# Long convolution of a 768-token mixer: two channel tiles by ScalarE products and adding DMAs, and the layer norm's steps placed between the blocks of the last mixing projection

## What is computed

```python
def conv_mixers(h, w_in, conv_a, conv_b, conv_b_bias, ln_g, ln_b, w_out):
    p = h @ w_in                                   # 1024 -> 5 x 512
    g_b, g_c, u_a, v_b, gate_b = jnp.split(p, ...)
    y_a = g_b * dwconv(g_c * u_a, conv_a)          # 3 taps
    u = v_b * jax.nn.sigmoid(gate_b)
    u = dwconv(u, conv_b) + conv_b_bias            # 31 taps, 512 channels
    y_b = jax.nn.silu(layernorm(u, ln_g, ln_b))    # over the 512 channels
    return jnp.concatenate([y_a, y_b], axis=-1) @ w_out
```

## Time and profile before

| what | value |
|---|---|
| median of 3 runs | 2915.93 us (2907.51 to 2917.44) |
| the profiled execution's own time | 2914.16 us |
| its span, first to last instruction | 2912.0 us |
| mean granted TensorE clock | 0.983 |
| PE busy | 2784.3 us (96%) |
| DVE busy | 1778.3 us (61%) |
| ACT busy | 1115.3 us (38%) |
| adding DMAs (`sw_vb<-tap_prod`) | 29, 391.5 KB each, median 5.2 us from issue to landing |

### The profile page before, as it was taken

The page is one execution under the profiler, slowest core; times in us unless marked ns, Lnnn a source line. Parts: engine busy times, 40 slices in busy tenths (PEclk is TensorE's granted clock), DMA queues, the critical chain, the costliest instruction groups (busy, mean ns, idle before and its releaser), DMA issues.

```text
span 2912.0 us, 41332 instructions
## 1 busy us (share of the span) xinstructions
PE 2784.3 (96%) x14371; PEld 2313.7 (79%) x14371; DVE 1778.3 (61%) x2765; ACT 1115.3 (38%) x1869; POOL 162.4 (6%) x205
## 2 busy tenths in 40 slices
PE   7998999999778999999998999999999998999998
PEld 6886788888676788887887888888888887788886
DVE  6775577676664677767885653453456655564645
ACT  5554322224664322223433332231224666352432
POOL 4211000001110000000210000000000000000000
PEclk8999999999998999999998999999999999999999
DMA  3211355452001344542651112112111000232322
GB/s 129 66 44 66 116 174 181 166 178 75 30 30 58 139 172 166 181 152 71 147 131 44 51 59 72 58 58 69 56 56 44 15 30 18 78 101 87 98 90 66
DMA packets 75217, 263.70 MB, mean 91 GB/s; under 512 B 8496, under 2 KB 10800, under 8 KB 73264
## 3 DMA queue, kind: packets, MB, share of 16 engines
q1 hardware_dynamic: 70880, 249.99, 25.5%
q0 software_dynamic: 4176, 11.63, 2.2%
HBM read 247.87 MB, written 2.10 MB: 86 GB/s over the span
## 4 chain that ended last, share of the span: by engine, by line
PE 67%; issue 16%; DVE 11%; ACT 4%; DVEq 2%; POOLq 0%; POOL 0%; ACTq 0%
PE psum L1942 18%; PE psum L1943 17%; PE psum L1944 17%; PE psum L2092 2%; DVE work L1471 1%; PE psum L2070 1%; PE psum L2341 1%; PE psum L2071 1%; ACT work L1101 1%; PE psum L2072 1%; DVE w_lo L1299 1%; ACT sw_pt L1113 1%; DVE work L1589 1%; DVE neg_max L1832 1%; PE psum L2329 1%
## 5 line engine op out<-in xcount | busy, mean ns | idle before, releaser
L1942 PE MATMUL psum<-hx_hi,w_hi 128*128 128x512 f32 x1568 | 624.6, 398 | 3.8 <-DVE hx_lo L1583 1.2
L1943 PE MATMUL psum<-hx_lo,w_hi 128*128 128x512 f32 x1568 | 622.0, 397 | 0.0
L1944 PE MATMUL psum<-hx_hi,w_lo 128*128 128x512 f32 x1568 | 621.3, 396 | 0.0
L759 ACT ACTIVATE w_hi<-w_raw 128x1024 fp32r<-128x1024 f32 (+1 forms) x328 | 344.8, 1051 | 515.1 <-PE psum L1944 207.5
L1299 DVE TENSOR_TENSOR w_lo<-w_raw,w_hi 128x1024 fp32r<-128x1024 f32 (+1 forms) x328 | 398.2, 1214 | 188.9 <-ACT w_hi L759 170.8
L1944 PEld LDWEIGHTS psum<-hx_hi,w_lo 128*128 128x128 f32 x1568 | 295.1, 188 | 72.0
L1942 PEld LDWEIGHTS psum<-hx_hi,w_hi 128*128 128x128 f32 x1568 | 295.3, 188 | 62.8 <-DVE hx_lo L1583 4.6
L1943 PEld LDWEIGHTS psum<-hx_lo,w_hi 128*128 128x128 f32 x1568 | 295.1, 188 | 47.5
L1942 PE MATMUL psum<-a_hi,w_hi 128*128 128x512 f32 (+1 forms) x656 | 234.6, 358 | 9.5 <-DVE a_lo L1411 9.0
L1943 PE MATMUL psum<-a_lo,w_hi 128*128 128x512 f32 (+1 forms) x656 | 234.5, 357 | 0.0
L1944 PE MATMUL psum<-a_hi,w_lo 128*128 128x512 f32 (+1 forms) x656 | 234.3, 357 | 0.0
(11 more groups left out here) (310 smaller groups left out, 4909.0 us busy)
## 6 DMA issues: line engine op xcount, KB each, us to landing
mod_w<-in_w_mod SPq DMA_DIRECT2D x96, 512.0 KB, 3.7
w_raw<-in_fup SPq DMA_DIRECT2D x88, 512.0 KB, 4.6
w_raw<-in_cup SPq DMA_DIRECT2D x88, 512.0 KB, 3.6
w_raw<-in_fdown SPq DMA_DIRECT2D x32, 512.0 KB, 4.8
w_raw<-in_cdown SPq DMA_DIRECT2D x32, 512.0 KB, 3.6
sw_vb<-tap_prod POOLq DMA_DIRECT2D x29, 391.5 KB, 5.2
w_raw<-in_da_qkv SPq DMA_DIRECT2D x18, 512.0 KB, 3.7
w_raw<-in_fdown SPq DMA_DIRECT2D x16, 384.0 KB, 3.3
```

Source lines behind the costliest of these rows:

```text
L759: r = act.activation(w_hi[:, off:off + n], w_raw[:, raw:raw + n], ACT.Copy)
L1942: pe.matmul(dst, wh, xh, start=first, stop=False)
L1943: pe.matmul(dst, wh, xl, start=False, stop=False)
L1944: return pe.matmul(dst, wl, xh, start=False, stop=last)
```

## The change

Three things are changed.

1. ScalarE and the adding DMAs now do tile 1 (31 taps) and, of tile 3, taps 10 to 30 (`SUM_TILES`). VectorE keeps tiles 0 and 2 and the first 10 taps of tile 3. A table, `PRODUCTS`, gives the products of each of 12 steps: steps 0 to 3 lie behind the last four blocks of `mix_c`, steps 4 to 11 behind the eight blocks of `mix_a`. Steps 0 to 3 have 3 products each, of tile 1; steps 4 to 11 have 6, 6, 6, 5, 5, 4, 4 and 4, of which the first part is of tile 1 and the second of tile 3. Each tile has two sums and 3 product buffers. The first two products of a tile go straight into its sums, the others are added by a DMA, so there are 48 adding DMAs instead of 29.
2. VectorE does 72 taps itself instead of 93, all of them ahead of `mix_b`, and in block 0 of `mix_b` adds up the sums (`conv_sums`) before it evacuates that block.
3. The blocks of `mix_b` are multiplied one after another (`mix_last`), not the first two side by side, in two of the four PSUM areas that blocks otherwise take in turn, and TensorE does the means behind block 0, the squares behind block 1 and the roots behind block 2. The other engines' steps of the layer norm are placed in the evacuation of the same blocks. The output projection takes k in the order 0, 1, 2, 4, 5, 6, 7, 3.

```diff
-SUM_TILE = 1
-TAP_BUFS = 4
+OWN_TAPS = [(q, j) for q, n in ((0, TAPS), (2, TAPS), (3, 10)) for j in range(n)]
+SUM_TILES = {1: 0, 3: 10}
+TAP_BUFS = 3
...
+def product_order():
+
+    steps, at = [], dict(SUM_TILES)
+
+    def take(q, n):
+        got = [(q, j) for j in range(at[q], min(at[q] + n, TAPS))]
+        at[q] += len(got)
+        return got
+
+    for b in range(12):
+        steps.append(take(1, 3 if b < 7 else 2) + (take(3, 3 if b < 9 else 2) if b >= 4 else []))
+    return steps
...
-    layernorm = dict(kind="layernorm", lin0=n["lin"], tile0=n["tile"])
-    stages.append(layernorm)
+    stages.append(dict(kind="layernorm"))
     n["tile"] += 4
-    add("resid", KT_D, k=KT_D, toks=ALL, w="w_out", src="A", gates=(0, 16), squares=ALL, ready=4)
-    layernorm["after"] = stages[-1]
+    add("resid", KT_D, k=KT_D, toks=ALL, w="w_out", src="A", gates=(0, 16), squares=ALL,
+        order=(0, 1, 2, 4, 5, 6, 7, 3))
...
+            return ps_lin(s % 2 if st["kind"] == "mix_b" else s, a, b)
...
-                    for j in range(2, TAPS):
-                        pool.wait_ge(s_tapp, j + 1)
-                        if j >= 4:
-                            pool.wait_ge(s_taps[j % 2], taps_added(j - 2))
-                        pool.dma_start(tap_sum(j % 2), tap_prod[:, j % TAP_BUFS, 0:TAP_COLS], accum_op=ALU.add)\
-                            .then_inc(s_taps[j % 2], 16)
+                    for n, (q, j) in enumerate(PRODUCT_LIST):
+                        at = j - SUM_TILES[q]
+                        if at < 2:
+                            continue
+                        pool.wait_ge(s_tapp, n + 1)
+                        if at >= 4:
+                            pool.wait_ge(s_taps[q][sum_of(q, j)], taps_added(q, j - 2))
+                        pool.dma_start(tap_sum(q, sum_of(q, j)), tap_buf(q, j), accum_op=ALU.add)\
+                            .then_inc(s_taps[q][sum_of(q, j)], 16)
...
+            def tap_products(step):
+
+                for q, j in PRODUCTS[step]:
+                    at = j - SUM_TILES[q]
+                    u = padded(q)[:, j:j + TAP_COLS]
+                    w = vcol("conv_b", TAPS * q + j)
+                    if at >= 2 + TAP_BUFS:
+                        act.wait_ge(s_taps[q][sum_of(q, j - TAP_BUFS)], taps_added(q, j - TAP_BUFS))
+                    dst = tap_sum(q, at) if at < 2 else tap_buf(q, j)
                     if j == 0:
-                        act.activation(dst, u[:, j:j + TAP_COLS], ACT.Identity, scale=w, bias=vcol("conv_b_bias", SUM_TILE))\
-                           .then_inc(s_tapp, 1)
+                        act.activation(dst, u, ACT.Identity, scale=w, bias=vcol("conv_b_bias", q)).then_inc(s_tapp, 1)
                     else:
-                        act.activation(dst, u[:, j:j + TAP_COLS], ACT.Copy, scale=w).then_inc(s_tapp, 1)
+                        act.activation(dst, u, ACT.Copy, scale=w).then_inc(s_tapp, 1)
                     act.drain()
...
-                    tap_products(12 + 3 * b, 15 + 3 * b)
+                    if b == 0:
+                        act.wait_ge(s_ev, st["lin0"] + 4)
+                    tap_products(4 + b)
                 return f
 
             def evac_mix_b(st):
                 def f(b, s, i):
...
             def evac_mix_b(st):
                 def f(b, s, i):
+                    if b == 3:
+                        norm_outputs()
                     act.wait_ge(s_ev, b + (st["lin0"] + 5))
                     act.activation(a_hi[:, b, :], wk[:, 2 * (s % 2), 0:ALL], ACT.Copy).then_inc(s_ahi, 1)
                     act.drain()
+                    if b == 0:
+                        norm_squares()
...
-                    conv_taps(42 + 9 * b // 2, 42 + 9 * (b + 1) // 2)
+                    conv_taps(42 + 30 * b // 8, 42 + 30 * (b + 1) // 8)
...
+            def conv_sums():
+
+                for q, first in SUM_TILES.items():
+                    for c in range(2):
+                        dve.wait_ge(s_taps[q][c], taps_added(q, TAPS - 1 - (TAPS - 1 - first - c) % 2))
+                    parts = [tap_sum(q, 0), tap_sum(q, 1)] + ([wk[:, 3, 0:TAP_COLS]] if first else [])
+                    for a, e, c in segs(ALL):
+                        o = HALO * c
+                        r = dve.tensor_tensor(conv_out[:, q, a:e], parts[0][:, o + a:o + e], parts[1][:, o + a:o + e], ALU.add)
+                    if first:
+                        dve.drain()
+                        for a, e, c in segs(ALL):
+                            o = HALO * c
+                            r = dve.tensor_tensor(conv_out[:, q, a:e], conv_out[:, q, a:e], parts[2][:, o + a:o + e], ALU.add)
+                    r.then_inc(s_ln["conv"], 1)
+                    dve.drain()
...
             def evac_mix_b(st):
+                tile0 = st["tile0"]
+
                 def f(b, s, i):
+                    if b == 0:
+                        conv_sums()
+                    if b == 2:
+                        norm_mean_squares()
+                    if b == 3:
+                        norm_outputs(tile0)
                     t = wk[:, 2 * (s % 2), 0:ALL]
                     dve.wait_ge(s_mm, b + (st["block0"] + 1))
-                    dve.tensor_tensor(t, ps_lin(s), conv_a[:, b, :], ALU.mult).then_inc(s_ev, 1)
+                    dve.tensor_tensor(t, ps_of(st, s), conv_a[:, b, :], ALU.mult).then_inc(s_ev, 1)
+                    dve.drain()
+                    low_part(b, t, ALL, tile0 + (b + 1 if b < 3 else 8))
                     dve.drain()
                     if b == 0:
-                        for c in range(2):
-                            dve.wait_ge(s_taps[c], taps_added(TAPS - 1 - c))
-                        for a, e, c in segs(ALL):
-                            o = HALO * c
-                            r = dve.tensor_tensor(conv_out[:, SUM_TILE, a:e], tap_sum(0)[:, o + a:o + e],
-                                                  tap_sum(1)[:, o + a:o + e], ALU.add)
-                        r.then_inc(s_ln["conv"], 1)
-                        dve.drain()
-                    low_part(b, t, ALL, b + (st["tile0"] + 1))
-                    dve.drain()
-                    conv_taps(78 + 4 * b, min(82 + 4 * b, 93))
+                        norm_centers()
...
-                pair(st["after"], 0, 4)
+            def norm_means():
...
+            def mix_last(st):
+                for s, inside in enumerate((norm_means, norm_squares, norm_roots, None)):
+                    pe.wait_ge(s_lo, st["block0"] + s + 1)
+                    pe.wait_ge(s_ev, st["lin0"] + (s + 1 if s < 2 else s + 3))
+                    for k in range(KT_D):
+                        step(st, s, k)
+                    if s == 0:
+                        pe.wait_ge(s_ev, st["lin0"] + 4)
+                    if inside is not None:
+                        inside()
...
+                    if st["before"]["kind"] == "mix_b":
+                        pe.wait_ge(s_ev, st["lin0"] + 4)
+                for at in range(k0, k1):
+                    k = st["order"][at] if st.get("order") else at
+                    operand(st, at)
```

More of the change, by code:

```diff
@@ L54 @@
 ROW, ROW_N = offsets(ROW_COLS)
+def product_order():
[7 more added lines that the diff above has]
+    return steps
+PRODUCTS = product_order()
+PRODUCT_LIST = [tap for step in PRODUCTS for tap in step]
+assert len(PRODUCT_LIST) == sum(TAPS - first for first in SUM_TILES.values())
 def make_plan():
@@ L188, in program @@
         w_raw = sbuf("w_raw", [P, 4 * D])
+        tap_space = ExitStack()
+        _, tap_prod3, _, tap_sum3 = (sbuf(name, shape, F32, tap_space) for name, shape in (
+            ("tap_gap", [P, 4 * D]), ("tap_prod3", [P, 2, D]), ("tap_gap2", [P, 4 * D]), ("tap_sum3", [P, 2, D])))
+        tap_space.close()
         w_hi = sbuf("w_hi", [P, 6 * D], F32R)
@@ L311, in program @@
         s_tapp = sem("tap_product_ready")
-        s_taps = [sem(f"tap_added_to_sum{c}") for c in range(2)]
+        s_taps = {q: [sem(f"tap_added_to_sum{c}_of_tile{q}") for c in range(2)] for q in SUM_TILES}
         s_const = sem("constants_ready")
@@ L892, in f @@
                         act.drain()
[L893 to L897, removed]
-                return f
[L900 to L904, removed]
-                    act.activation(wk[:, j % 2, 0:ALL], conv_out[:, j, :], ACT.Square).then_inc(s_ln["sq"], 1)
-                    act.drain()
-                for j in range(4):
-                    act.wait_ge(s_ln["t"], j + 1)
-                    act.activation(wk[:, 2 + j % 2, 0:ALL], wk[:, j % 2, 0:ALL], ACT.Silu,
-                                   bias=vcol("ln_bias", j)).then_inc(s_ln["s"], 1)
-                    act.drain()
-                    act.activation(a_hi[:, 4 + j, :], wk[:, 2 + j % 2, 0:ALL], ACT.Copy).then_inc(s_ahi, 1)
-                    act.drain()
+                    if b == 4:
+                        act.wait_ge(s_ev, st["lin0"] + 8)
+                    if b >= 4:
+                        tap_products(b - 4)
```

(15 more changed lines are left out.)

59 lines of the change are left out of this document (38 added, 21 removed).

## The result

| what | before | changed |
|---|---|---|
| median | 2915.99 us (4 runs) | 2953.80 us (4 runs, 2947.93 to 2956.61) |
| ratio to before, 95% interval | | 1.0129 (1.0113 to 1.0145) |
| the profiled execution: time, span, clock | 2914.16, 2912.0, 0.983 | 2955.53, 2953.6, 0.974 |

The changed kernel is 37.8 us slower by the medians; the forecast was 2951 us, 35 us above the median of before (36.9 above its profiled execution). The mixer stage takes nearly all of it: from the root of the norm ahead of it to the root of the norm behind it (POOL's `tok_r`) it lasts 318.9 us instead of 284.2 us.

A forecast was written before the change was run, and what follows sets the result against it. TensorE set the pace up to 1520 us; after the change the DMA engines bound `conv_out`, whole at 1537.5 us. Plus 70.4 us, the pair ends at 1607.9, 36.9 later: 2914.2 + 36.9 = 2951 us, range 2933 to 2970.

The forecast's parts named there:

- The price of an add: Each adding DMA within SBUF occupies all 16 DMA engines for 2.26 us.
- The last add: Behind mix_a's blocks, the last adding DMA lands at 1535.3 us, at a DMA share of 1.03.
- an engine works at one packet at a time: Reading of the DMA share, never much above 1.09 in the busiest slices.
- Late weights: Roundings queue behind products, so TensorE stalls some 7 us in mix_a or at mix_b; costed at nothing.
- From `conv_out` to the pair's end: TensorE's means, three blocks, squares, spreading, wait, w_out's first pair and half clock take 70.4 us.
- the wait before w_out: TensorE waits 5.4 us for PSUM areas, since VectorE evacuates block 3 only behind the norm's outputs.
- the mark (X): End of w_out's first pair, forecast to move from about 1571 to 1607.9 us; X is w_out's first block.
- 31.2 us: TensorE's full-clock work from 1521.3 to 1571 us before the change; the other 18.5 us are waits and half clock.
- The product waits: Sign: ScalarE's products wait 60 us or more for adds, where it was 18.5.
- The rival "hidden", 2905 us: Adds of different sums overlap in the DMA engines and land in time: 8 to 10 us faster; chance 0.06.
- The threshold of 1.4 us per add: An add of about 1.4 us means no change, with `conv_out` whole at 1503.3 us.
- The rival "starved": POOL's one issue order starves the DMA queue, share 0.87: 54 us slower, 2968 us; chance 0.12.

The follow-up runs named there:

- plain copies: Changed kernel with the 48 adding DMAs copying the product over the sum instead of adding it: 2924.19 us, ratio 1.0019.
- adds alone: Changed kernel's 48 adding DMAs, but norm, mix_b and w_out in the order of before, sums behind block 0's evacuation: 2936.13 us, ratio 1.0063.
- norm alone: Changed kernel with the norm between the blocks, but taps 10 to 30 of tile 3 left out and 29 adding DMAs: 2915.91 us, ratio 1.0003.
- half adds: Changed kernel with each adding DMA adding only the first 391 of 783 columns: 2929.15 us, ratio 1.0043.
- sums first: Changed kernel with 29 adds, tile 3 cut to 2 taps, last three taps and sums ahead of mix_a's last short convolution: 2909.08 us, ratio 0.9962.
- alternating order: Changed kernel with the products of a step alternating between tiles 1 and 3, on ScalarE and in POOL's queue: 2945.31 us, ratio 1.0111.
- fewer taps: Changed kernel with 29 adds and tile 3 cut to its first 2 taps, so VectorE does 64 taps: 2917.47 us, ratio 1.0001.
- late adds by a table: Kernel before, with the last 11 taps of tile 3 as late products, 9 more adding DMAs, norm unmoved: 2914.84 us, ratio 0.9997.
- the last four taps: Kernel before with 11 late tile 3 products, norm's steps inside w_out's first pair, VectorE's last four taps in its wait for ScalarE's copy: 2905.31 us, ratio 0.9958.

## Why the prediction was right, and where it wasn't

- *The price of an add* (2.26 us of 16 engines) held: 2.22. *The last add* was forecast at 1535.3 us; VectorE's sum, which waited for it, began at 1536.50. `conv_out` was whole at 1538.63 us, forecast 1537.5. This term carries the result, and the shares of 0.99 and 1.05 bracket the 1.03 taken. That "an engine works at one packet at a time" is not shown: shares of 1.05 over 40 us are already more than that would give. Only the level is.
- The Trainium skill, page "DMA: Bandwidth & Descriptors", section "Bandwidth", gives some 435 GB/s as the ceiling between SBUF and SBUF. The plain copies come near it (0.4009 MB in 1.06 us are 378 GB/s); the adds move 181 GB/s. So the copy is within the ceiling, and the ceiling is no price of an add.
- *Late weights*: 8.1 us of stalls for the 7 forecast, 5.67 for a `w_lo` and 2.45 for an evacuation by VectorE (`work`, line 1550), which itself had stood 7.76 us for a rounding. Block 0 of `mix_b` ended at 1508.9 instead of 1503 us: the stage began 2.1 us later, and the first stall was followed by half clock (0.58 from 1486.7 to 1493 us). TensorE's delay was covered by the wait for `conv_out`, 29.89 us for "some 30". That such stalls cost when the cover is gone, "adds alone" shows: 18.4 us, not 7. What the forecast did not have is that late roundings hold up VectorE's own way to the sums.
- *From `conv_out` to the pair's end* 70.4 us were forecast; from 1538.63 to 1608.4 us are 69.8. The means took 7.61 us (8.15 forecast with their half clock), the squares 8.24 (7.3, with the half clock booked on block 2), the wait before w_out 6.67 (5.4). From the start of the means to the mark (X) it is 68.8 us here, 69.3 in "norm alone", 68.9 with half adds and 69.3 with copies: the term does not depend on the adds. It does depend on the clock: 69.9 in "sums first", 67.1 in "alternating order", and 65.1 in "fewer taps".
- That this sum comes out so close is partly luck. The forecast calls 7.3 us of squares and 1.55 us of spreading work at full clock, but both rows ran below it (0.70 and 0.50). At a clock of 0.99 the squares took 5.41 us ("fewer taps"), and the spreading took 0.82 us here at 1.00. So the sum has some 2.6 us too much of work, which a wait before w_out that is 1.3 us longer and a little more half clock make up for; its "31.2 us" of work at the full clock is too high by the same.
- *The product waits* were a sign that did not come: ScalarE waited 32.2 and 4.5 us for the two sums, not 60 or more. With the roundings and evacuations it was busy for 45.8 of the 90 us from 1442 to 1532, of which the 40 products at 0.952 us, 38.1 us, could have been counted ahead.
- *The rival "hidden", 2905 us*, was wrong in its size. The step that failed is "block 0 of `mix_b` ends at 1495.8 with `conv_out` whole". It does end there (1495.31), but VectorE's tail makes `conv_out` whole 8 us later, and the mark comes 69.3 us behind the means and not 65 to 68 (which "fewer taps" and "alternating order" did reach). 1503.5 + 69.3 = 1572.8: no gain. The threshold of 1.4 us per add falls with it: at 1.24 us the kernel is 0.43%, at 1.06 us 0.19% slower than before. The threshold has only the last landing in it, and VectorE's program was late by then.
- *The rival "starved"* did not come: the share was 0.99 and 1.05, not 0.87. Its mechanism shows in "alternating order", with some 5 us in one profile, which the medians don't confirm.

What stays open: how much of a shorter wait the clock takes back, and where the rest of the gain is from ("sums first"); what the norm's place does with VectorE's taps as before; and why the late `w_lo` appears in "late adds by a table".

## What to carry to other kernels

Cost a DMA that accumulates from a row that shows one, not from its bytes, and count the engines' time of all of them before moving work there: here the bound went from VectorE to the DMA engines and stayed where it was. A full DMA queue reaches further than its last landing: the products wait for it, the roundings stand behind the products, and VectorE behind the roundings. Before a consumer is moved up, look what stands in the producer's program ahead of its last step; moving four taps into a wait shortened the stage by 4.1 us, moving the norm's steps into the pair by 4.9. The costs of two edits don't simply add: the new order of the norm turns a late sum into a delay of everything behind it, where the old one still had work to put in front.

## What the runs showed of the hardware

- An accumulating DMA from SBUF to SBUF of 391.5 KB takes 2.22 us of the 16 engines and 144 packets; one of half the columns takes 1.24 us and also 144 packets; a plain copy of the whole takes 1.06 us and 80 packets.
- After a wait of 3 to 30 us the sum over `conv_out` took 6.9 to 8.3 us of TensorE, without one 5.3 to 5.9. A wait of 3.90 us (8.31, "the last four taps") cost no less of the clock than one of 29.89 us (7.61, the changed kernel).
- At a granted clock of 1.00 the matmul rate of the same long stage was not the same in every execution. The windows from 1700 to 2100 us, first of before, then of the last kernel (PE x2265 and x2294):

```profile
1700.00:2100.00 400.00, 400.00 (x2265) 348.42 (x2264) 175.33 (x234) 104.09 (x110) 0.00 (x0) 1.00 0.19 62
```

```profile
1700.00:2100.00 400.00, 400.00 (x2294) 350.91 (x2294) 179.82 (x239) 106.25 (x112) 0.00 (x0) 1.00 0.19 63
```

It is 1.3%, some 6 us between the roots around that stage (574.0 and 567.6 us). Of the twelve traces here eleven have 574.0 us and 2265 to 2267 matmuls; the one that differs is that of the last kernel, so 6.4 us of what its profile gains on the others lie in a stage that no edit touches. A single profile can't tell smaller differences of this kernel's whole time, and the medians are to be used. The cause stays open.
